# Values, output turns and the RWKV preparation moved to other places in the order of the sample attention loop

## The reference, cut to what matters

```python
def mla_attend(q_lat, q_pe, q_pos, c_kv, k_pe, k_pos, w_uv):
    s = (einsum('bthc,bsc->bhts', q_lat, c_kv) + einsum('bthr,bsr->bhts', q_pe, k_pe)) * MLA_SCALE
    s = where(k_pos[None, :] <= q_pos[:, None], s, -inf)
    p = softmax(s, axis=-1)
    o_lat = einsum('bhts,bsc->bthc', p, c_kv)
    return einsum('bthc,chv->bthv', o_lat, w_uv)
# RWKV preparation
prev = concatenate([shift0[:, None, :], rw[:, :-1]], axis=1)
xs = rw + (prev - rw) * mu                    # split into r, k, v, xw, xa, xg
w_log = -softplus(-(w0 + tanh(xw) @ w2)) - 0.5; decay = exp(-exp(w_log))
a = sigmoid(a0 + xa @ a2);  g = sigmoid(xg) @ g2
kk = k * k_k; kk = kk / max(sqrt(sum(kk * kk, -1)), 1e-12)
k = k * (1 + (a - 1) * k_a)
y, S = rwkv7_scan(r, decay, k, v, -kk, kk * a, S0)
```

## Time and profile before

| | us |
|---|---|
| median of 3 runs | 1773.77 |
| the other two runs | 1771.05, 6021.15 |
| the profiled execution | 1773.77 |
| its span, first to last instruction | 1772.1 |
| sample attention block up to the end of low_rank(7) | 169.5 to 270.2 |
| RWKV preparation up to the first pairs | 270.2 to 297.9 |

### The profile page before, as it was taken

How to read it: one execution, slowest core, us unless ns; L and a number is a source line. 1 busy time by engine, 2 the same in 40 slices (tenths; PEclk the granted TensorE clock), 3 DMA queues, 4 the chain that set the end, 5 groups by cost and what they waited for, 6 DMA issues and landing times.

```text
span 1772.1 us, 43013 instructions
## 1 busy us (share of the span) xinstructions
PE 1691.5 (95%) x19692; PEld 1120.5 (63%) x19692; DVE 640.8 (36%) x1169; ACT 332.4 (19%) x542; POOL 98.2 (6%) x149
## 2 busy tenths in 40 slices
PE   6998998998999999989999999999999999999994
PEld 6966776988999999968435344353443534447342
DVE  5537648648655448556420120100101111011111
ACT  3222234024433334434100000000000000000001
POOL 0026310000000000000000000000000000010100
PEclk8999998989999999999899999999999999999997
DMA  9244640017544435164999999999999999997995
GB/s 290 66 137 112 192 105 1 3 45 222 165 145 143 154 109 158 58 212 135 359 411 417 416 416 417 414 418 414 417 417 405 417 407 414 417 397 313 416 407 207
DMA packets 173689, 477.03 MB, mean 269 GB/s; under 512 B 31290, under 2 KB 115804, under 8 KB 142612
## 3 DMA queue, kind: packets, MB, share of 16 engines
q1 hardware_dynamic: 169038, 459.87, 68.4%
q0 software_dynamic: 4272, 14.36, 2.5%
q10 hardware_dynamic: 198, 0.05, 0.0%
HBM read 461.54 MB, written 15.83 MB: 269 GB/s over the span
## 4 chain that ended last, share of the span: by engine, by line
PE 51%; DMA 2%; SPq 2%; DVE 1%; issue 0%; ACT 0%; POOL 0%; POOLq 0%; ACTq 0%; DVEq 0%
PE bank L2680 46%; DMA ring<-in_moe_w_down 1%; SPq L2339 1%; PE bank L327 1%; PE bank L328 1%; PE bank L329 1%; SPq L2343 1%; PE bank L2531 0%; PE bank L2654 0%; DMA ring<-y_rows_dram,y_index 0%; PE bank L2617 0%; PE bank L2546 0%; PE bank L2610 0%; PE bank L2550 0%; PE bank L2565 0%
## 5 line engine op out<-in xcount | busy, mean ns | idle before, releaser
L2680 PE MATMUL bank<-ring,x 128*32 128x512 f32 (+1 forms) x6144 | 586.6, 540 | 2.5 <-DMA ring<-in_moe_w_gu 2.1
L2680 PEld LDWEIGHTS bank<-ring,x 128*32 128x32 f32 x6144 | 204.6, 110 | 353.6 <-issue 333.7
L2680 PE MATMUL bank<-ring,hid 128*32 128x256 f32 x5376 | 292.0, 379 | 0.1
L2680 PEld LDWEIGHTS bank<-ring,hid 128*32 128x32 f32 x5376 | 183.9, 110 | 108.3 <-issue 2.5
L327 PE MATMUL bank<-x_hi,w_hi 128*128 128x320 f32 (+1 forms) x488 | 152.5, 313 | 0.0
L328 PE MATMUL bank<-x_lo,w_hi 128*128 128x320 f32 (+1 forms) x488 | 151.4, 310 | 0.0
L329 PE MATMUL bank<-x_hi,w_lo 128*128 128x320 f32 (+1 forms) x488 | 151.4, 310 | 0.0
L2148 DVE TENSOR_TENSOR w_lo<-ring,w_hi 128x2048 fp32r<-128x2048 f32 (+2 forms) x51 | 112.5, 2208 | 96.7 <-ACT w_hi L2070 96.5
L3033 DVE TENSOR_TENSOR hrow<-sil,bank 128x512 f32<-128x512 f32 (+1 forms) x48 | 26.9, 616 | 300.7 <-PE bank L2680 300.7
L2070 ACT ACTIVATE w_hi<-ring 128x2048 fp32r<-128x2048 f32 (+2 forms) x51 | 94.1, 1846 | 128.2 <-PE bank L329 125.8
L2805 ACT ACTIVATE sil<-bank 128x512 f32<-128x512 f32 (+1 forms) x48 | 22.6, 544 | 453.1 <-PE bank L2680 453.1
(11 more groups left out here) (581 smaller groups left out, 2123.7 us busy)
## 6 DMA issues: line engine op xcount, KB each, us to landing
ring<-in_moe_w_gu SPq DMA_DIRECT2D x128, 1024.0 KB
ring<-in_moe_w_down SPq DMA_DIRECT2D x112, 1024.0 KB
ring<-in_moe_w_gu SPq DMA_DIRECT2D x128, 768.0 KB
ring<-in_ffn_w_gu_even SPq DMA_DIRECT2D x44, 512.0 KB, 4.9
ring<-in_w_in_odd SPq DMA_DIRECT2D x12, 1024.0 KB, 5.5
ring<-in_ffn_w_down_even SPq DMA_DIRECT2D x10, 1024.0 KB, 5.6
proj_ring<-in_w_in_even SPq DMA_DIRECT2D x9, 1024.0 KB, 7.4
pages<-in_cache_mla SPq DMA_DIRECT2D x56, 144.0 KB
```

The lines of the kernel that those rows point to most:

```text
L2680: mm = t.matmul(ps[banks[g3]][SL * y:SL * y + SL, 0:w], act[:, g3, k, :], m_ring[:, slot, at + y * w:at + (y + 1) * w], start=start, stop= ...
```

## The change

It puts the same operations into another order and changes the waits that go with it; no operation is added or removed, and the arithmetic is the same.

1. In the sample loop, TensorE's pass `b` now begins with scores(b + 1), which also waits for the exponentials of `b` (they read the banks that it writes). values, new_values and turn_out come one pass later: pass `b` has turn_out(b - 2), values(b - 1, 0), values(b - 1, 1), new_values(b - 1). What is left of them at the end follows the loop.
2. ScalarE's pass has out_cols(b - 2) first, then the two copies, then exponentials(b + 1), `part`, the copy of turn_new, out_row(b - 1).
3. VectorE's maximum(b + 1) stands ahead of gap(b). Ahead of it stand all six turns in pass 0, four in pass 1, one from then on; the others are spread behind.
4. ov goes to the upper half of bank 7 and is copied (with `ov_taken`) by VectorE behind the norms. The turned `vT` of the third tile waits for that copy, where it waited for the last out_row.
5. In the preparation, VectorE takes the norms' maxima (which need L1181) first, and the scans behind them. TensorE's gate product stands ahead of the spread norms.
6. All of `pairs` waits for the bonus (`bonus_ready`), where only the third tile did. The gate's sigmoid goes to the head of ScalarE's second list. The buffers `uv` and `rx` are placed elsewhere in SBUF.

The core of the diff (TensorE's loop, VectorE's loop, ScalarE's loop, then the preparation):

```diff
@@ scores, other_max, both_totals, turn_out
                                 t.wait_ge(pg_turned, NT * (b - 1))
+                            t.wait_ge(ex_ready, b)
...
-                            t.wait_ge(weight_ready, b)
+                            if b >= 2:
+                                t.wait_ge(ol_ready, b - 1)
+                            else:
+                                t.wait_ge(weight_ready, b)
...
-                            t.wait_ge(ol_ready, b)
+                            t.wait_ge(new_taken, b + 1)
...
-                            t.wait_ge(*((new_taken, b + 2) if b + 1 < NB else (weight_ready, NB)))
+                            t.wait_ge(weight_ready, min(b + 2, NB))
+                            t.wait_ge(ol_ready, b)
@@ TensorE, the loop
                         for b in range(NB):
+                            if b + 1 < NB:
+                                scores(b + 1)
+                            if b >= 2:
+                                turn_out(b - 2)
                             turn_probs(b)
                             other_max(b)
+                            if b:
+                                values(b - 1, 0)
                             if b == NB - 1:
                                 turn_shift()
-                            else:
-                                scores(b + 1)
                             turn_new(b)
-                            values(b, 0)
                             if b:
-                                turn_out(b - 1)
-                            if b == NB - 1:
-                                for n in range(4):
-                                    low_rank(n)
-                            values(b, 1)
-                            new_values(b)
+                                values(b - 1, 1)
+                                new_values(b - 1)
                             both_totals(b)
+                        turn_out(NB - 2)
+                        values(NB - 1, 0)
+                        for n in range(4):
+                            low_rank(n)
+                        values(NB - 1, 1)
+                        new_values(NB - 1)
                         for n in range(4, 8):
                             low_rank(n)
@@ VectorE, the loop
                         for b in range(NB):
+                            ahead = (NT, 4, 1)[min(b, 2)]
+                            turns(b + 2, range(ahead))
+                            if b + 1 < NB:
+                                maximum(b + 1)
+                            turns(b + 2, range(ahead, 2))
                             v.wait_ge(other_full, b + 1)
...
-                            turns(b + 2, range(2))
+                            turns(b + 2, range(max(ahead, 2), 4))
                             v.wait_ge(part_ready, b + 1)
...
-                            turns(b + 2, range(2, 4))
-                            if b + 1 < NB:
-                                maximum(b + 1)
-                            turns(b + 2, range(4, NT))
+                            turns(b + 2, range(max(ahead, 4), NT))
@@ VectorE, the preparation
+                            v.wait_ge(kk_full, 1)
+                            v.tensor_scalar(rn[:, 0:2, :], ps[4][:, 0:2 * RH]..., 1e-24, None, ALU.max)
+                            v.tensor_scalar(rn[0:64, 2, :], ...).then_inc(kk_var, 1)
+                            v.wait_ge(lo_act, 4)
                             for c in range(4):
-                                v.wait_ge(lo_act, c + 1)
                                 last = v.tensor_tensor_scan(t4[:, c, :], ...)
...
+                            v.wait_ge(ov_full, 1)
+                            v.tensor_copy(mixT[:, 0:4, SEQ:TOK], VAL[:, 256:512]...).then_inc(ov_taken, 1)
                             v.wait_ge(lo_act, 8)
-                            v.wait_ge(v_full, NB)
@@ TensorE, the preparation
                                 if i == 2:
-                                    t.wait_ge(o_ready, NB)
+                                    t.wait_ge(ov_taken, 1)
...
+                            t.wait_ge(tg_ready, 2)
+                            for c in range(4):
+                                t.wait_ge(lo_act, 5 + c)
+                                t.matmul(ps[c][:, 0:TOK], g2[:, c * P:(c + 1) * P], sg[:, :], ...).then_inc(lo_full, 1)
                             t.wait_ge(kk_var, 1)
                             t.wait_ge(v_taken, 3)
@@
                             t.wait_ge(ar_ready, 1)
+                            t.wait_ge(bonus_ready, 1)
                             t.wait_ge(st_free, NB)
```

More of the change, by code:

```diff
@@ L1008, in model @@
                     g2 = sbuf(st, "g2", [P, RDIM])
+                    rx = sbuf(st, "rx", [P, 3, RH, RD])
                     tw = sbuf(st, "tw", [64, TOK])
@@ L1262, in _ @@
                         for b in range(NB):
+                            if b >= 2:
+                                out_cols(b - 2)
                             for k in range(2):
@@ L1275, in _ @@
                             if b:
-                                out_cols(b - 1)
-                            if b + 1 < NB:
-                                exponentials(b + 1)
-                        for n in range(8):
+                                out_row(b - 1)
+                        out_cols(NB - 2)
+                        for n in range(4):
                             log_decay(n)
-                        s.activation(sg[:, :], rwT[:, 13, :], ACT.Sigmoid).then_inc(tg_ready, 1)
                         out_row(NB - 1)
+                        for n in range(4, 8):
+                            log_decay(n)
                         out_cols(NB - 1)
@@ L1444, in _ @@
                                 mm.then_inc(bc_full, 1)
-                            t.wait_ge(tg_ready, 2)
-                            t.wait_ge(ov_taken, 1)
-                            for c in range(4):
-                                t.wait_ge(lo_act, 5 + c)
-                                t.matmul(ps[c][:, 0:TOK], g2[:, c * P:(c + 1) * P], sg[:, :], start=True, stop=True).then_inc(lo_full, 1)
                             t.wait_ge(bo_ready, 1)
```

25 lines of the change are left out of this document (10 added, 15 removed).

## The result

The changed kernel took 1789.13 us in the median (1783.65 to 1800.74, 20 runs), the kernel before 1775.54 beside it (20 runs, 1771.05 to 1784.15 without one of 6021.15). The ratio is 1.0082, with a 95% interval of 1.0067 to 1.0096: some 14 us slower, which is within 2%, as forecast, and outside the range of the prediction. The direction was right, the size was twice the forecast.

What follows compares the result with a forecast made beforehand. TensorE was taken to fill the steady loop, 11.05 us a pass without waits, and VectorE's chain to set the end behind it. 5.3 to kk's last product plus 1.1 for pairs gave +6.4, from 1773.8 to 1780.2 us; range 1772 to 1787.

Steps and rivals of the forecast that it cites:

- The pages: 0, but barely: Sample loop: page loads and turns need 11.8 to 14.5 us against 13.9 available, so no delay; upper bound 5 us.
- rival "late pages": Sample loop: rounds 4 to 7 wait in VectorE's turns, up to +5 on the +6.4, 1781 to 1785; 17 in 100.
- Doubled for queueing: Sample loop's page loads: upper bound of 0.6 us a round over four rounds, doubled, giving 5 us.
- rival "second clock loss": Pass 0 or 1: the new 2.5 us pause brings another stretch at 1.2 GHz, +3.4, 1783.6; 10 in 100.
- The steady loop, 0: Sample loop: the new order's chain of 11.06 us ties with TensorE's 11.05, so no delay; at most 1 us over five passes.
- The first pass, +2.5 of idle time: First loop pass: TensorE has only 1.1 us of work behind scores(1), then about 2.5 us of new idle time.
- The last pass, +0.8: Last loop pass: turn_out(6) stands right behind both_totals(7) and new_values(6), with out_row(6) between; about 0.8 us idle.
- L1181 ends 2.5 later: Behind the loop: the sums of `kk * kk` on TensorE end at 276.4, against 273.9 before.
- The scans lose their cover: Preparation, VectorE: the scans, which ran under L1181, now wait behind the norms' maxima; scans and difference take 4.5 us.
- The spread norms at 1.2 GHz: Preparation, TensorE: gate product 4.43 us, then spread norms 3.98, both at 1.2 GHz; last product of kk +5.3.
- the rival "the clock stays at 2.4 GHz behind the loop": Preparation, TensorE: at the full clock the delay is +2.7 in all, 1776.5 us; 17 in 100.
- pairs, +1.1: Preparation: all pairs wait for the bonus, so VectorE waits for 32 of 80 matmuls that took 2.84 us, 1.1 us.

Runs made afterwards that it cites:

- the kernel without loads: The changed kernel with the page transfers of sequences 4 to 7, and the waits for them, left out: 1781.40 us, ratio 1.0036.
- the kernel with all the repairs: The changed kernel with quad 1 issued by ScalarE, scans ahead of the wait for L1181, only the third tile of pairs waiting for the bonus: 1786.04 us, ratio 1.0053.
- The kernel with seven fillers: The kernel before plus unread matmuls: four behind scores(0), one ahead of the sums of `kk * kk`, two ahead of the spread norms: 1767.97 us, ratio 0.9960.

## Why the prediction was wrong

The step that failed is **"The pages: 0, but barely"**, with the rival built on it. It had 11.8 to 14.5 us of need against 13.9. Its terms, as measured: the issue of twelve transfers 6.4 to 6.7 (forecast 6.3); the landing 6.4 (3.9 to 5.1); the turns behind the late quad 3.1 (211.59 to 214.74; 1.56 to 3.1). The need is 16.0. The available time was 13.8: from 198.7 to 212.5, where scores(4) would have started, 11.05 behind 201.46. So it is 2.2 short, and the wait was 2.30. Two things were wrong in it. The landing was mis-sized: I had read it from one round. The next round of the kernel before (transfers issued 203 to 206) has

```profile
DMA to landing us min/median/max: 4.0/4.4/5.6
```

and with 5.6 the sum would have been 15.0. The new order also brings the reload of the queries next to SP's quads and GpSimd's quad 3, where the prediction had "no other traffic"; but the engines were at 1.00 in the kernel before and at 0.99 now, so that this is what made 6.4 of 5.6 is not shown. And the zero was the wrong choice between the ends: the page is complete only with its last transfer and the work behind it, so the maxima belong in the sum, and by my own terms these gave 14.5, already more than 13.9. "Doubled for queueing" was applied to the wait and not to the landing.

The price of the **rival "late pages"** (up to +5) was too low, because it counted waits alone. Two long passes cost 8.4. The scores at 1.2 GHz are 4.6 of it (6.65 and 5.40 for 3.71), the waits of TensorE 3.55 (1.08 + 1.15 and 0.17 + 1.15). The **rival "second clock loss"** was thought of in passes 0 and 1 and priced at 3.4. There it came too, at 1.7: scores(2) took 5.40 behind the waits of 0.93 and 1.50. It has nothing to do with the pages, for without the loads scores(2) took 5.02. What I had kept as separate cases of 17 and 10 in 100 came together, and the late pages brought a clock loss of their own. The prediction named late pages together with a clock loss as what its range left out.

The other steps, by the distance from the maximum of sequence 0:
- *The steady loop, 0*: right. It is 11.0 a pass without the loads.
- *The first pass, +2.5 of idle time*: right, 0.93 + 1.50 = 2.43.
- *The last pass, +0.8*: 0.50 twice for out_row.
- *L1181 ends 2.5 later*: 12.5 later in the changed kernel, 2.5 in the kernel without loads. The step was right apart from the pages.
- *The scans lose their cover*: right that they run bare, 1.5 by itself.
- *The spread norms at 1.2 GHz*: wrong. The gate product took 2.32, where 4.43 was taken over, and the spread norms 2.84 with a wait of 0.19 in it (296.08 to 298.92), where 3.98 was. The clock there was 0.98 (292.8 to 299.7); the rival "the clock stays at 2.4 GHz behind the loop" was right for these two. The preparation came out below its terms: from the end of the sums of `kk * kk` to the masked pairs it is 26.7 against 25.1 before, +1.6, where the prediction had +3.9 (6.4 less 2.5).
- *pairs, +1.1*: the wait was 2.24, because 32 matmuls behind a wait of 4.59 ran at 1.2 GHz. I had taken the price from a row at 2.4 GHz.

The sum: forecast +6.4; up to the end of the sums of `kk * kk` +10.0 (12.5 less 2.5), of which 8.4 are the pages with their clock and 1.6 the first two intervals, which differ between executions; the preparation -2.3 (1.6 less 3.9); together +14.1, with +14.0 measured. The +6.4 itself was right only as a sum, which is luck: the kernel without loads has +5.2 by the trace and +6.3 by the median, with the clock loss in pass 1 and the pairs dearer and the preparation cheaper than forecast.

Open is what lengthens the landing from 5.1 (5.6 in the next round) to 6.4. Taking a third of the issues off SP and half of the bytes away did not end the waits.

## What to carry to other kernels

When buffers come free later, add up issue, landing and the work behind the landing against the time that is left, and take the slowest landing of all rounds, since the change itself moves the transfers together; when the upper end of that sum is more than the time there is, the wait is a term and not a rival. Price a new wait on TensorE with the clock behind it: in the changed kernel the two waits of 2.23 and 1.32 us cost another 2.94 and 1.69 in the scores that followed. A wait that cannot be removed can be filled with matmuls that nothing reads; it paid where nothing else was late, and where the pages were late no gain could be measured.

## What the runs showed of the hardware

- Transfers of 144 KB landed in 2.1 us at best and in 6.4 at worst within 15 us of the changed kernel (issued 198 to 213); the slowest was issued while the engines were at 0.99. A full engine does not settle it: in the kernel before, transfers issued 203 to 206 at a share of 1.00 landed in 4.0 to 5.6 us.
- A transfer of half the partitions took longer to issue on SP (468 ns against 332), so less data did not mean less queue time.
- The granted clock fell to 1.2 GHz behind pauses of 1.08 and 1.15 us close together, and of 0.17 and 1.15, in a loop that was otherwise full. It did not always: in the kernel with all the repairs the scores took 3.71 us at a clock of 1.00 behind pauses of 1.04 and 1.15, and 5.40 behind 0.70 and 1.14. It did not fall either where quad 3 is turned first, with pauses of 0.30, 1.08 and 0.20 ahead of the scores. The Trainium skill (TensorE: Matmul & The Clock Gate, "What's actually happening") has it that the throttled state is the default and activity releases it. The kernel with seven fillers agrees: 0.52 became 1.00.
- Seven idle-filling matmuls, in a kernel whose trace counts some 19,700 matmul instructions, made it 0.4% faster.
